# Attention over cached keys: pages transposed by VectorE in 32x32 blocks instead of by TensorE, and scores computed chunk by chunk

## The chip, the cores and the metric
The program runs on one core of a Trainium2 chip. The metric is the device time of one execution in microseconds (us); lower is better. Everything is float32.

## What is computed
One inference step of a small decoder: a pooling layer with its mixture of experts (MoE), then shared keys, values and forget gates, then one attention layer with its MoE. The prompt has 528 rows; 8 sample sequences have 4 new rows each and 2048 past rows in a paged cache of keys and values (16 pages of 128 rows, 16 heads of 64, so a page is 128 x 1024 floats, 512 KB). What the change touches is the attention of the samples over their past:

```python
s_past = jnp.einsum('nqhd,nkhd->nhqk', q, k_past).astype(jnp.float32) * ATTN_SCALE
s_past = s_past + cq - c_past.transpose(0, 2, 1)[:, :, None, :]
...
p = jax.nn.softmax(jnp.concatenate([s_past, s_new], axis=-1), axis=-1)
out = jnp.einsum('nhqk,nkhd->nqhd', p[..., :past].astype(v_past.dtype), v_past)
return out + jnp.einsum('nhqk,nkhd->nqhd', p[..., past:].astype(v_new.dtype), v_new)
```

## The kernel before, in words
The stages follow one another: pooling, MoE, projections (keys, values, queries), attention, output projection, second MoE. Each engine has its own program, and semaphores tie them together.

The attention stage is a loop `attention(i)` over the 8 samples, written out once for i = 0 and then as a hardware loop. Each round of it does three things, interleaved by hand in numbered ticks (`TICKS`, `S_TICK`, `QK_TICK`, `O_TICK` and so on say at which tick each engine writes which step):
- the front of sample i: its keys are brought into a layout in which 64 head dimensions lie on the partitions, and the scores of its 16 query rows per head group are computed and masked into `SROW`;
- the back of sample i - 1: softmax over `SROW`, transposes of the probabilities (`p_transposes`), products with the values (`values`);
- two heads of the prompt's attention (`s_step`, `t_step`, `v_step`; softmax by `pmax`, `exp`, `pnorm`; `pts` copies transposed probabilities out of PSUM).

Keys come in chunks of four pages into `KB`, which holds two chunks; values go to four slots `VSL`. SyncE (SP in the profile) issues these loads in `load_chunk`: for each page it reads the page's number from the table into a register, then issues one DMA for the 128 rows of 4 KB. `attention_loads` is a fixed order: wait until chunk ch has left `KB` (semaphore `kt_tr`), load the chunk two further on, wait for `pv_done`, load value chunk ch; the bias rows (`load_bias`) go in between. GpSimd (POOL) issues the loads of the prompt's heads (`stage`).

In `k_tick` (L1110) TensorE transposes 128x128 blocks of keys, 4 in a tick and 32 ticks a round. VectorE (`evac` on even ticks, L1933) and ScalarE (on odd ticks, L1491) copy them from PSUM to `KTR`. `qk` (L1128) multiplies them with `QBLK`, the block of queries, 256 columns at a time in four column tiles. The prompt's rows of the last tile of queries and keys go from ScalarE into `QT4` and `KT4` (parts of `KQ4`), separate from the buffer `TS` of the earlier tiles.

## Time and profile before

| | |
|---|---|
| time, median of 3 runs | 1629.07 us (1629.01 to 1629.26) |
| the profiled execution: its own time | 1625.25 us |
| its span in the profile | 1623.5 us |
| mean granted TensorE clock | 0.945 of full speed (2.4 GHz) |
| busy: PE (TensorE matmuls), DVE (VectorE), ACT (ScalarE), POOL (GpSimd) | 90%, 29%, 20%, 7% |
| DMA over the span | 424.59 MB, mean 262 GB/s |

The attention stage lies from about 662 to about 1200 us. In rows of stretches, "DMA share" is the mean busy share of the 16 DMA engines and GB/s what they moved; the rate at a full share is the one divided by the other. PEld are TensorE's weight loads, SPq and ACTq what the SyncE and ScalarE queues issue.

### The profile page before, as it was taken

The page shows a single profiled execution, that of the slowest core. Times are in us where ns is not written, and L with a number is a line of the kernel's source. Part 1 is how long each engine was busy: PE and PEld are TensorE (multiplying, and loading weights), DVE is VectorE, ACT ScalarE, POOL GpSimd, SP SyncE. Part 2 cuts the span into 40 slices and gives each one's busy share as a digit, 9 for nine tenths or more (in the row PEclk, how much of TensorE's full clock was granted, in tenths as well). Part 3 has the DMA queues.
Part 4 walks back from the last instruction along what each step waited for, and adds up shares of the span by engine and source line. Part 5 has one row for each costly group of instructions (what it writes and reads, how often), then busy time and mean ns, then how long its engine had stood idle before and what let it go on. Part 6 is the DMA issues. An engine that isn't in the chain of part 4 may idle for free.

```text
span 1623.5 us, 37862 instructions
## 1 busy us (share of the span) xinstructions
PE 1455.5 (90%) x15152; PEld 1040.5 (64%) x15152; DVE 471.8 (29%) x1112; ACT 328.7 (20%) x696; POOL 118.5 (7%) x176
## 2 busy tenths in 40 slices
PE   4988999999399999589999999999999599999991
PEld 4877988888244444356555656655545488888881
DVE  3330010000122332365545555555413301000103
ACT  2120110111111111333333434433211011110110
POOL 1012000000200000101001000000000210000002
PEclk9789999999799999799999999999998699999995
DMA  8256999999931131677988987987753069999975
GB/s 245 125 217 205 390 393 390 377 381 395 327 135 41 38 102 38 210 249 258 317 280 275 314 294 269 316 280 277 296 233 136 20 215 397 388 386 397 394 280 182
DMA packets 121996, 424.59 MB, mean 262 GB/s; under 512 B 26519, under 2 KB 40920, under 8 KB 113471
## 3 DMA queue, kind: packets, MB, share of 16 engines
q1 hardware_dynamic: 90439, 367.60, 61.8%
q0 software_dynamic: 10448, 29.73, 6.1%
q10 hardware_dynamic: 21040, 26.29, 4.7%
q8 instruction: 49, 0.80, 0.2%
q14 instruction: 20, 0.16, 0.0%
HBM read 393.70 MB, written 30.24 MB: 261 GB/s over the span
## 4 chain that ended last, share of the span: by engine, by line
PE 59%; DMA 16%; issue 14%; DVE 4%; ACT 3%; SPq 3%; POOL 1%; ACTq 1%; DVEq 0%; POOLq 0%
DMA W<-in_w_up 14%; PE PS L969 10%; PE PS L856 6%; PE PS L1110 6%; PE PS L852 6%; PE PS L887 4%; PE PS L882 4%; PE PS L1176 3%; PE PS L1128 3%; PE PS L1094 3%; PE PS L791 3%; PE PS L1055 2%; PE PS L1075 1%; DMA KB<-yd,SLi 1%; SPq L396 1%
## 5 line engine op out<-in xcount | busy, mean ns | idle before, releaser
L852 PE MATMUL PS<-W,VB 128*32 128x384 f32 x3072 | 353.2, 492 | 15.7 <-DMA W<-in_w_up 6.7
L856 PE MATMUL PS<-W,VB 128*32 128x128 f32 x3072 | 352.0, 275 | 5.5 <-issue 5.4
L856 PEld LDWEIGHTS PS<-W,VB 128*32 128x32 f32 x3072 | 335.3, 111 | 11.6 <-issue 9.6
L882 PE MATMUL PS<-W,VB 128*32 128x384 f32 x1536 | 174.7, 492 | 5.6 <-ACT VB L1326 5.6
L1110 PE MATMUL PS<-C,KB 128*128 128x128 f32 x1024 | 168.5, 296 | 9.4 <-ACT W L1491 7.7
L887 PE MATMUL PS<-W,VB 128*32 128x128 f32 (+1 forms) x1024 | 174.7, 329 | 0.0
L1110 PEld LDWEIGHTS PS<-C,KB 128*128 128x128 f32 x1024 | 118.4, 148 | 74.8 <-issue 59.8
L1755 DVE TENSOR_TENSOR VB<-VB,PS 128x384 f32<-128x384 f32 x32 | 17.7, 554 | 511.4 <-PE PS L868 470.5
L852 PEld LDWEIGHTS PS<-W,VB 128*32 128x32 f32 x3072 | 144.5, 110 | 28.8 <-DMA W<-in_w_up 12.2
L887 PEld LDWEIGHTS PS<-W,VB 128*32 128x32 f32 x1024 | 102.2, 110 | 16.0 <-issue 0.2
L1491 ACT ACTIVATE W<-PS 128x512 f32<-128x512 f32 x128 | 76.1, 595 | 169.4 <-PE PS L1110 164.2
L1933 DVE COPY W<-PS 128x512 f32<-128x512 f32 x128 | 88.1, 688 | 60.6 <-PE PS L1110 58.7
L882 PEld LDWEIGHTS PS<-W,VB 128*32 128x32 f32 x1536 | 72.4, 110 | 29.6 <-issue 20.9
L969 PE MATMUL PS<-W,VB 128*128 128x512 f32 x192 | 85.6, 603 | 1.5 <-DVE VB L1605 1.5
L1128 PE MATMUL PS<-W 128*32 128x256 f32 x1024 | 83.8, 400 | 2.2 <-DVE W L2028 1.4
L969 PE MATMUL PS<-W,KB 128*128 128x512 f32 x192 | 83.8, 593 | 0.0
L791 PE MATMUL PS<-C,VB 96*128 96x96 f32 (+2 forms) x376 | 52.7, 284 | 34.3 <-DVE VB L1586 24.0
L791 PEld LDWEIGHTS PS<-C,VB 96*128 96x128 f32 (+2 forms) x376 | 45.5, 191 | 41.9 <-DVE VB L1586 24.4
L1055 PE MATMUL PS<-W 65*128 65x128 f32 (+4 forms) x160 | 64.0, 483 | 5.4 <-DMA W<-out_v_prompt 5.4
L1094 PE MATMUL PS<-W 128*64 128x128 f32 (+2 forms) x480 | 62.6, 260 | 4.2 <-DVE W L1973 3.1
L969 PEld LDWEIGHTS PS<-W,VB 128*128 128x128 f32 x192 | 36.6, 194 | 45.5 <-issue 45.5
L1332 ACT ACTIVATE VB<-PS 128x768 f32<-128x768 f32 x32 | 26.0, 812 | 192.7 <-PE PS L887 192.7
(261 smaller groups left out, 1589.9 us busy)
## 6 DMA issues: line engine op xcount, KB each, us to landing
W<-in_w_gate SPq DMA_DIRECT2D x32, 2048.0 KB
W<-in_w_up SPq DMA_DIRECT2D x32, 2048.0 KB, 21.6
W<-in_w_down SPq DMA_DIRECT2D x32, 2048.0 KB, 11.3
KB<-in_cache_k SPq DMA_DIRECT2D x128, 512.0 KB, 5.2
W<-in_cache_v SPq DMA_DIRECT2D x64, 512.0 KB, 5.5
VB<-in_cache_v SPq DMA_DIRECT2D x64, 512.0 KB, 7.3
yd<-VB ACTq DMA_DIRECT2D x32, 288.0 KB, 7.0
W<-in_w_kvf SPq DMA_DIRECT2D x4, 2048.0 KB, 15.7
```

Source lines behind the costliest of these rows:

```text
L791: mm = pe.transpose(PS[:, bank + k // 4, (k % 4) * P:(k % 4) * P + r], s, ident[0:r, 0:r])
L852: pe.matmul(PS[32 * q:32 * q + 32, bank, 0:WIDE], x, w[:, k, 0:WIDE], start=(k == 0), stop=(k == KC - 1), tile_position=(0, 32 * q), skip_ ...
L856: mm = pe.matmul(PS[CAP:P, bank, P * q:P * q + P], x, w[:, k, WIDE:FF], start=(k == 0 and q == 0), stop=(k == KC - 1), tile_position=(0, C ...
L882: pe.matmul(PS[32 * q:32 * q + 32, 5 + n, 0:WIDE], h, w[:, f, n * WIDE:n * WIDE + WIDE], start=(f == 0), stop=(f == FC - 1), tile_position ...
L887: mm = pe.matmul(PS[CAP:P, b, at:at + n], h, w[:, f, rest + lo:rest + lo + n], start=(f == 0 and at == 0), stop=(f == FC - 1), tile_positi ...
L969: mm = pe.matmul(PS[0:r, b, :], x[:, k, 0:r], wv[s][:, k, :], start=(k == 0), stop=(k == KC - 1))
L1055: pe.matmul(PS[0:r, 6, 0:nk], QST[hh][0:DH + 1, t * P:t * P + r], KST[hh][0:DH + 1, 0:nk], start=True, stop=True)
L1094: mm = pe.matmul(out, VST[0:kr, j, vc], PTS[0:kr, j * r:(j + 1) * r], start=(j == 0), stop=(j == t), tile_position=(0, DH * hh))
L1110: mm = pe.transpose(PS[:, n % 2, (2 * x + g) * P:(2 * x + g + 1) * P], ks[:, 2 * half + g, hp * P:(hp + 1) * P], ident)
L1128: mm = pe.matmul(PS[32 * a:32 * a + 32, 2, 256 * half:256 * half + 256], QBLK[:, 2 * a + j, :], KTR[:, (2 * x + a // 2) % 4, 256 * (a % 2) ...
L1491: act.activation(KTR[:, n % 4, :], PS[:, n % 2, :], ACT.Copy).then_inc(sem("kt_odd"), 1)
L1933: dve.tensor_copy(KTR[:, n % 4, :], PS[:, n % 2, :]).then_inc(sem("kt_even"), 1)
```

## The change
- **Loads.** A key page is loaded by four DMAs instead of one. DMA a brings heads 4a to 4a + 3 (256 columns, runs of 1 KB) of all 128 rows to the 32 partitions 32a to 32a + 31; row 32c + t goes to partition t of the group, piece c. The page numbers of a chunk are read with one register load, for values too. SyncE's wait before a key load is now for the chunk's scores (`qk_done`).
- **Transposes.** `k_tick`, both `evac` and `KTR` are gone. VectorE transposes a page in place in 32x32 blocks (`keys_transposed`, 16 instructions of 128x1024 a round, on even ticks), after waiting for the whole chunk at its first page.
- **Scores.** `qk` runs once a chunk: 8 matmuls of 512 columns in four column tiles straight from `KB`, where the 128 rows of the contraction are 4 heads' 32 dimensions each, against a block-diagonal `QBLK`. The score rows of a column tile now belong to heads a, a + 4, a + 8, a + 12, and bias, values and outputs follow that order.
- **Moved.** `pts` goes from VectorE to ScalarE; `values` runs per chunk and not per page, ahead of `qk`; the output is copied twice (`OB` has 512 columns) and transposed four times instead of twice; the new rows' scores have 32 columns instead of 64.
- **Last tile.** The last tile of queries and keys uses `TS` like the others, so ScalarE waits for `ktd_out` and `qtd_out` (the stores of what `TS` held) there too. VectorE makes the samples' own `KQR` and transposes it (`K4T`, `Q4T`).

```diff
-KTICKS = 32
-QK_TICK = [2 * x + 3 for x in range(KTICKS // 2)]
+K_TICK = [2 * g for g in range(PAGES)]
+QK_TICK = (7, 15, 23, 31)
+SCORE_TICK = (8, 16, 24, 32)
-O_TICK = [g + 8 for g in range(PAGES + 1)]
+O_TICK = (7, 15, 23, 29)
...
-            def load_chunk(dst, rows, i, ch, s):
-                for g in range(CH):
-                    page = sp.value_load(pt[0:1, bass.ds(i * PAGES + ch * CH + g, 1)], min_val=0,
-                                         max_val=A["cache_k"].shape[0] - 1)
-                    sp.dma_start(dst[:, g * D:(g + 1) * D], rows[bass.ds(page * PAGE, PAGE), :]).then_inc(s, 16)
+            def load_chunk(dst, rows, i, ch, s, keys=False):
+                pages = nc.values_load_multi_w_load_instructions(
...
+                for g, page in enumerate(pages):
+                    src, to = rows[bass.ds(page * PAGE, PAGE), :], dst[:, g * D:(g + 1) * D]
+                    if keys:
+                        for a in range(4):
+                            sp.dma_start(to[32 * a:32 * a + 32, :].rearrange("p (c f) -> p c f", c=4),
+                                         src[:, 256 * a:256 * a + 256].rearrange("(c t) f -> t c f", t=32)).then_inc(s, 16)
...
-                    sp.wait_ge(sem("kt_tr"), 32 * i + 8 * (ch + 1))
+                    sp.wait_ge(sem("qk_done"), 4 * i + ch + 1)
...
-                def k_tick(n):
...
-                    for x in range(2):
-                        hp = 4 * m + 2 * x + j
-                        for g in range(2):
-                            mm = pe.transpose(PS[:, n % 2, (2 * x + g) * P:(2 * x + g + 1) * P],
-                                              ks[:, 2 * half + g, hp * P:(hp + 1) * P], ident)
-                    mm.then_inc(sem("kt_tr"), 1)
...
+                def qk(ch):
+
+                    pe.wait_ge(sem("kt_done"), 16 * i + CH * ch + CH)
...
+                    ks = KB[:, ch % 2, :].rearrange("p (x n) -> p x n", n=256)
+                    for e in range(2):
+                        for a in range(4):
+                            b = 2 * a + e
+                            mm = pe.matmul(PS[32 * a:32 * a + 32, ch % 2, :], QBLK[:, b, :], ks[:, :, 32 * b:32 * b + 32],
+                                           start=(e == 0), stop=(e == 1), tile_position=(0, 32 * a), skip_group_check=True)
...
-                dst = TS if t < 4 else QT4
-                if t < 4:
-                    act.wait_ge(sem("ktd_out"), 32 * (t + 1))
+                dst = TS
+                act.wait_ge(sem("ktd_out"), 32 * (t + 1))
...
+                def keys_transposed(g):
+
+                    ch = g // CH
+                    if g % CH == 0:
+                        dve.wait_ge(sem(f"k_in{ch % 2}"), 256 * (2 * i + ch // 2 + 1))
+                    page = KB[:, ch % 2, g % CH * D:g % CH * D + D]
+                    dve.transpose(page, page).then_inc(sem("kt_done"), 1)
```

**SyncE's queue in the hardware loop,** at the load of a key chunk. Before, each page has a register load, its checks and one DMA (two pages shown of four):

```order
L495 ISA [waits kt_tr]
L495 TENSOR_LOAD pt
L495 ISA x2
L497 ISA
L497 DMA KB<-in_cache_k 128x1024
L495 ISA
L495 TENSOR_LOAD pt
```

Now, with one register load for the chunk:

```order
L498 ISA [waits qk_done]
L498 TENSOR_LOAD pt
L505 ISA
L505 DMA KB<-in_cache_k 32x4x256
L505 ISA
L505 DMA KB<-in_cache_k 32x4x256
```

The last two rows go on until there are 16 DMAs, where there were 4; the row that waits stands in front of the value chunk and the bias rows that follow it.

**TensorE in the loop,** four ticks of it. PS is PSUM, C holds the identity, W the carved buffers (`KTR`, `QBLK`, `PR`). Before:

```order
L1110 MATMUL PS<-C,KB 128x128 [waits kt_odd]
L1110 MATMUL PS<-C,KB 128x128 x3
L1128 MATMUL PS<-W 32x256 [waits s_ready,kt_odd,kt_even]
L1128 MATMUL PS<-W 32x256 x3
L1110 MATMUL PS<-C,KB 128x128 [waits kt_even]
L1110 MATMUL PS<-C,KB 128x128 x3
L1075 MATMUL PS<-C,W 128x128 [waits pu_pts,pu_norm]
L1075 MATMUL PS<-C,W 128x128 x2
L1055 MATMUL PS<-W 128x512 [waits pu_exp]
```

Now, around the scores of a chunk:

```order
L1165 MATMUL PS<-W 32x256 x15
L1112 ISA
L176 ISA [waits qb_ready,kt_done]
L1122 MATMUL PS<-KB,W 32x512 [waits s_ready]
L1122 MATMUL PS<-KB,W 32x512 x7
L1083 REGISTER_ALU
L1087 MATMUL PS<-C,W 128x128 [waits pu_pts,pu_norm]
L1087 MATMUL PS<-C,W 128x128
L1067 MATMUL PS<-W 128x384 [waits pu_exp]
```

The L1110 rows of every tick are gone, and the score matmuls (L1128 before, L1122 now) stand in one block of 8 behind a wait for VectorE's transposes.

**VectorE in the loop,** where the last chunk of a sample begins, now:

```order
L1954 STREAM_TRANSPOSE KB<-KB 128x1024 [waits k_in1]
L1986 REGISTER_ALU
L1988 ISA [waits qk_done]
L1992 ISA [waits bias_in0]
L1994 TENSOR_TENSOR W<-PS,BIAS 128x512 [waits ptt_tr]
L1998 TENSOR_REDUCE W<-W 128x1 [waits s_ready]
L1961 REGISTER_ALU
L1964 TENSOR_REDUCE W<-PS 128x1 [waits pu_exp,pu_s]
L1954 STREAM_TRANSPOSE KB<-KB 128x1024
L1980 RECIPROCAL W<-W 128x1 [waits pu_exp]
L1982 TENSOR_SCALAR W<-W 128x512 [waits pu_rec]
```

The wait for the loaded chunk (`k_in1`) is now VectorE's, with the prompt's softmax rows (L1964 on) queued behind it; before it was TensorE's.

## Rows read from the trace of the kernel before

**Rows 1.** The page's head and its part on the 40 slices.
```profile
PE   4988999999399999589999999999999599999991
...
PEclk9789999999799999799999999999998699999995
```

**Rows 2.** Windows, one per round of the loop: busy us (count), PEclk, DMA share, GB/s.
```profile
685.90:747.80 61.90, 56.99 (x486) 38.08 (x486) 38.51 (x95) 24.75 (x63) 4.76 (x8) 0.97 0.75 257
747.80:809.60 61.80, 59.12 (x560) 35.74 (x559) 32.08 (x83) 23.21 (x58) 4.76 (x8) 0.97 0.85 281
933.40:995.30 61.90, 59.99 (x562) 36.71 (x562) 32.95 (x85) 23.19 (x58) 4.75 (x8) 0.97 0.85 294
1057.40:1119.40 62.00, 59.32 (x556) 35.31 (x554) 32.11 (x84) 23.02 (x58) 4.75 (x8) 0.97 0.85 291
```

**Rows 3.** The chain that ended last, 871 to 934 us, its first lines.
```profile
by line: PE PS L1110 21.9%; PE PS L1176 14.7%; PE PS L1128 11.8%; PE PS L1094 10.1%; PE PS L1055 9.2%; issue 7.5%; PE PS L1075 4.0%; PE PS L1158 3.5%; PE PS L1058 1.8%; DVE W L1943 1.6%; DVE W L1933 1.3%; ACT W L1501 1.3%; DVE W L1989 1.1%;
...
877.42 0.59 PE PS L1110 x4
878.01 0.57 PE PS L1128 x8
```

**Rows 4.** Groups by line and shape: out<-in, count, busy us, mean ns, idle before.
```profile
L1491 ACT ACTIVATE W<-PS 128x512 f32<-128x512 f32 x128 | 76.1, 595 | 169.4 <-PE PS L1110 164.2 <-issue 5.2
L1933 DVE COPY W<-PS 128x512 f32<-128x512 f32 x128 | 88.1, 688 | 60.6 <-PE PS L1110 58.7
```

**Rows 5.** Timeline of VectorE before the stage: start, us, what.
```profile
602.62 1.22 DVE L1877 TENSOR_TENSOR VB<-VB,kgb 128x1024 f32<-128x1024 f32 x1
```

**Rows 6.** Windows of DMA traffic; columns as in Rows 2.
```profile
604.70:606.20 1.50, 1.50 (x5) 0.64 (x4) 0.00 (x0) 0.74 (x1) 0.00 (x0) 1.00 0.86 350
606.70:609.40 2.70, 2.70 (x8) 1.24 (x7) 0.00 (x0) 0.00 (x0) 0.00 (x0) 1.00 0.82 194
646.20:647.70 1.50, 1.50 (x10) 0.57 (x8) 0.00 (x0) 1.11 (x1) 0.00 (x0) 1.00 0.65 131
665.40:666.90 1.50, 0.30 (x2) 0.30 (x3) 0.00 (x0) 0.69 (x1) 0.00 (x0) 0.50 1.00 393
350.00:400.00 50.00, 49.46 (x797) 44.33 (x796) 4.73 (x9) 5.38 (x9) 1.11 (x2) 1.00 1.00 387
10.20:13.60 3.40, 1.52 (x7) 1.55 (x8) 1.45 (x2) 0.20 (x1) 1.36 (x3) 1.00 1.09 375
```

**Rows 7.** What SyncE issues, by source line: ns min/median/max, first and last start.
```profile
L497 SPq DMA_DIRECT2D KB<-in_cache_k x128: 331/333/348, 583.6 to 1137.0; - x128
L495 SPq TENSOR_LOAD <-pt x256: 262/268/1275, 582.7 to 1166.2; - x128
L541 SPq DMA_DIRECT2D KB<-in_w_o x2: 389/396/403, 1148.4 to 1162.4; - x2
L490 SPq DMA_DIRECT2D W<-in_w_kvf x4: 540/657/4670, 395.4 to 411.4; - x4
```

**Rows 8.** Timeline of SyncE's queue in one round.
```profile
962.34 3.85 SPq L497 DMA_DIRECT2D KB<-in_cache_k  x4
967.08 3.62 SPq L497 DMA_DIRECT2D VB<-in_cache_v  x4
...
981.02 3.62 SPq L497 DMA_DIRECT2D VB<-in_cache_v  x4
985.37 3.23 SPq L506 DMA_DIRECT2D BIAS<-rpd  x4
```

**Rows 9.** The chain that ended last, where the stage begins.
```profile
665.15 0.65 ACTq L1474
665.86 0.70 ACT KQ L1413
...
667.21 8.85 DMA qtd<-KQ
```

**Rows 10.** Line L1474 (the stores of keys): from DMA to landing.
```profile
DMA to landing us min/median/max: 3.2/3.6/5.4
```

More of the change, by code:

```diff
@@ new lines, in values @@
+                    pe.wait_ge(sem("ptt_ready"), 5 * i - 5 + ch + 1)
+                    pe.wait_ge(sem(f"v_in{ch}"), 64 * i)
+                    for g in range(CH):
+                        for a in range(4):
+                            v = paged(VSL[ch])[:, g, :].rearrange("p (x a d) -> p a x d", a=4, d=DH)[:, a]
+                            mm = pe.matmul(PS[32 * a:32 * a + 32, 5, 0:256], PTT[:, CH * ch + g, 32 * a:32 * a + 32], v,
+                                           start=(ch == 0 and g == 0), stop=False, tile_position=(0, 32 * a), skip_group_check=True)
@@ new lines, in values @@
+                    mm.then_inc(sem("pv_done"), 1)
+                    if ch == NCH - 1:
+                        pe.wait_ge(sem("ptt_ready"), 5 * i)
+                        settled(pe)
+                        for a in range(4):
+                            v = V4[S0:2 * S0, :].rearrange("p (x a d) -> p a x d", a=4, d=DH)[:, a]
+                            mm = pe.matmul(PS[32 * a:32 * a + 32, 5, 0:256], PTT[S0:2 * S0, PAGES, 32 * a:32 * a + 32], v,
+                                           start=False, stop=True, tile_position=(S0, 32 * a), skip_group_check=True)
+                        mm.then_inc(sem("o_mm"), 1)
@@ L1183, in attention, with out_transposes @@
+                def out_transposes():
+                    pe.wait_ge(sem("ob_ready"), i)
+                    pe.wait_ge(sem("sn_ready"), i + 1 if front else i)
+                    settled(pe)
+                    for a in range(4):
+                        at = (P - NS) * a
+                        mm = pe.transpose(PS[:, 2 if front else 7, at:at + P], OB[:, a].rearrange("p u d -> p (u d)"), ident)
+                    mm.then_inc(sem("ob_tr"), 1)
                 for n in range(TICKS + shift):
@@ L1506, in exp, with pts @@
                             .then_inc(sem("pu_exp"), 1)
+                def pts(u):
+                    t = u % 5
+                    act.wait_ge(sem("pu_t"), 10 * i + u + 1)
+                    after(act, sem("pu_v"), 10 * i + u)
+                    if t < 4:
+                        act.activation(PTS[:, 0:P * (t + 1)], PS[:, 7, 0:P * (t + 1)], ACT.Copy).then_inc(sem("pu_pts"), 1)
+                    else:
+                        r = LASTP
+                        act.activation(PTS[:, 0:4 * r], PS[:, 7, 0:4 * r], ACT.Copy)
+                        act.activation(PTS[0:r, 4 * r:5 * r], PS[0:r, 7, 4 * r:5 * r], ACT.Copy).then_inc(sem("pu_pts"), 1)
                 def ot(u):
```

214 lines of the change are left out of this document (90 added, 124 removed).

## The prediction, on record before the changed kernel ran
> **What bounds the kernel now.** The page's forty slices show TensorE busy at nine tenths almost throughout, at a granted clock near full [rows 1]. The windows then cut the attention stage into rounds of its loop. Seven of them, from 685.9 to 1119.4 us, are 61.8 to 62.1 us long [rows 2]. In a round TensorE is busy for some 60 us, VectorE for 32.9, ScalarE for 23.2 and the DMA engines for 0.85 to 0.87 of it. So TensorE sets the pace, but DMA is only a seventh behind it. The chain of one round says the same: of it TensorE's own lines are over three quarters, the key transposes (L1110) alone 21.9%, and no transfer is named [rows 3]. Since a quicker TensorE meets the loads soon, the price of the key loads decides this change.
>
> **TensorE.** The chain gives one tick of four transposes as 0.59 us and one group of four column tiles (L1128) as 0.57 us [rows 3]. There are 32 ticks, so 18.9 us leave each round. The scores are 16 groups of 256 columns now, 9.1 us, and become 8 groups of 512 columns. As many columns pass, with half as many starts, so between 8.0 and 9.1 us; I take 8.0. TensorE's floor is 61.9 - 18.9 - 1.1 = 41.9 us a round.
>
> **VectorE and ScalarE.** The copies out of PSUM go: 16 x 0.688 = 11.0 us of VectorE and 16 x 0.595 = 9.5 us of ScalarE [rows 4]. `pts` moves, about 4.7 us. Added are 16 transposes of 128x1024. The trace has no such instruction; the nearest is the 128x1024 multiply at 1.22 us [rows 5], 19.5 us a round. Below it I see no reason; above, I allow twice it, if a 4-byte block costs two passes. VectorE comes to 32.9 - 11.0 - 4.7 + 19.5 = 36.7 us (56 at most), ScalarE to about 19. Both are covered by what follows. The position costs more than the work: VectorE waits for the whole chunk at its first page, and the prompt's softmax is queued behind that wait. A late chunk therefore stops TensorE within a tick or two.
>
> **SyncE.** A chunk's four pages take 3.6 to 3.9 us to issue, and four bias DMAs 3.2 [rows 8]. A key DMA is 0.333 us, a table load 0.268 [rows 7]. The new key DMA has 32x4x256 elements. Rows with three dimensions lie at 0.396 us (128x8x512 from w_o) and 0.54 to 0.66 us (the same shape from w_kvf) [rows 7]. I take 0.39, since w_o's steps in memory are powers of two like the cache's. With some 0.07 us of register work each, a key chunk is 16 x 0.46 + 0.6 = 8.0 us, a value chunk 4 x 0.40 + 0.6 = 2.2. The round is 4 x 10.2 + 2 x 3.2 = 47 us. At 0.66 us a DMA it is 4 x 14.5 + 6.4 = 64 us, which would be a bound of its own.
>
> **The key transfers.** A round moves 294 GB/s x 61.9 us = 18.2 MB [rows 2], of which keys are 16 x 0.524 = 8.4 MB. In a long saturated stretch 387 GB/s at a share of 1.00 pass [rows 6], so the rest, 9.8 MB, needs 25.3 us. For the keys three prices are in [rows 6], each the rate divided by the share. The best is that of the start, 10.2 to 13.6 us, where pool_w with its runs of 1 KB (256 floats) was among the traffic: 375 / 1.09 = 344 GB/s, 24.4 us. The worst is that of stores from few partitions. Storing 512 KB of keys from 128 partitions gives 350 / 0.86 = 407 GB/s; storing the same amount in two DMAs of 64 partitions each, one after the other, gives 194 / 0.82 = 237; and the 16 and 32 rows of the last tile give 131 / 0.65 = 202 GB/s, which is half. At that price keys need 41.5 us. But where such a store of 16 and 32 rows ran beside a 128-partition load, the window shows 393 GB/s at 1.00, so nothing was lost: the loss appears where all engines are in the same few partitions together. The four DMAs of a page go to four different groups, in order through one queue, and within a chunk there are sixteen. Engines that drift apart by a DMA or two are in different groups. I take the middle, 33 us. Sum 25.3 + 33.0 = 58.3 us, or 49.7 and 66.8 at the ends; with 3% of gaps, 60, 51 and 69.
>
> The trace's halved rate is what the Trainium skill, "SBUF — State Buffer", section "Door 1: The DMA port swizzle", states: 32 partitions reach 8 of 16 ports, measured there at 189 GB/s against 328, and two DMAs to the two halves don't add up. By the page alone keys would take 44 us and the round 70 us, slower than now. The 48-partition row agrees with it (202 GB/s); the mixed row is what it doesn't cover.
>
> **The ends.** In the last round the keys of a next sample aren't loaded, w_o's 4.2 MB are: 25.3 + 16.5 + 10.8 = 52.6 us, with gaps 54, so 8 us saved. At the start, ScalarE now waits for the key stores of the last tile before it scales the queries. The activation stood right behind the issue, at 665.86, and leads through an 8.85 us transfer to the first scores [rows 9]; the stores are issued until 665.80 and land in 3.2 to 5.4 us [rows 10], so between 668.4 and 670.6. Since the DMA engines were full there (share 1.00 in the fourth row of [rows 6]), I take 4 us on the chain. Everything from the output projection on is untouched.
>
> **Sum.** Six rounds (747.8 to 1119.4) x (60.1 - 61.9) = -11; first round about 0, since it waits on the same stores and loads; last round -8; start +4. That is -15 us. From the profiled execution's 1625.25 us this gives 1610; the median of the runs stands 3.8 us above that execution, so 1614 us.
>
> **Rivals.**
> - *The loads cost nothing extra.* Then keys are at 344 GB/s, DMA needs 51 us a round, SyncE 47 and TensorE 42: about 52 us. 6 x -9.9, first round -5, last -12, start +4: -72, or 1557 us. For it: the mixed row at 393 GB/s. Against it: every row in which one narrow DMA is alone.
> - *The engines stay in step and the narrow DMAs run at half rate.* The place is the key load of every chunk, 10.4 us for 2.1 MB at 202 GB/s instead of 5.2 or so. Rounds of 69 us: 6 x 7, first +7, last -4, start +4: +49, or 1678 us. It decides against the change as soon as the keys are slower than some 240 GB/s (60.0 - 25.3 = 34.7 us for 8.4 MB, the point at which a round is 61.9). For it: both narrow rows (237 and 202 GB/s) are below that. Against it: sixteen DMAs in a row, beside GpSimd's loads, give engines room to part.
> - *SyncE becomes the bound*, at 0.66 us a DMA: 64 us of issue and the waits in the same queue, 66 us a round. 7 x 4, last 0, start +4: +32, or 1661 us. For it: the w_kvf rows; against it: the w_o rows.
> - *The clock.* Where TensorE waited, between 685.9 and 809.6, the clock was still 0.97 [rows 2]. With 42 us of work in 60 it may be granted less: even at 0.75 its 42 us are 56, still covered, so this sharpens the slow cases only.
>
> **How the numbers follow.** DMA takes TensorE's place at nearly the same length: 0.34, itself 1595 to 1635. Loads cost nothing extra: 0.26. In step: 0.28. SyncE: 0.08. Others, among them VectorE's transposes at twice the price with the waits around them: 0.04. The range runs to both outer cases, 1557 to 1678; it leaves out the tips. What a measurement of this kernel can tell from no change is about 0.2%, 3 us. The middle case straddles 1629: 0.24 faster, 0.06 within, 0.04 slower. With the others: faster 0.24 + 0.26 + 0.03 = 0.53, same 0.06, slower 0.41.
>
> **What would show it.** The round's length; a DMA share near 1.0 in every round, at 300 GB/s; VectorE's waits at the first transpose of a chunk, ended by the load of the cache's keys; TensorE busy for about 42 us a round at full clock and a lower granted clock; transposes near 1.2 us; key DMAs issued at 0.39 us. If SyncE's row of sixteen is 12 us long and DMA is under 0.9, the queue was the bound. If rounds are near 52 us, narrow loads were not slow. I would be wrong in kind if a wait between VectorE, TensorE and ScalarE, and no transfer, set the round.

## The result, and the profile after

The changed kernel takes 1756.1 us (median of 4 runs, 1751.55 to 1759.8), the kernel before 1629.0 us (4 runs, 1623.0 to 1629.3). The ratio is 1.079 with a 95% interval of 1.075 to 1.083: 7.9% slower, 127 us. Forecast were 1614 us, with a range of 1560 to 1678. The profiled execution took 1751.55 us, its span is 1749.8, its mean granted clock 0.855 (before 0.945).

The page of the changed kernel, with the lines that answer to [rows 1], and the chain that ended last over the whole span:

```profile
span 1749.8 us, 34372 instructions
PE 1390.2 (79%) x13632; PEld 970.3 (55%) x13632; DVE 506.8 (29%) x1026; ACT 290.4 (17%) x672; POOL 118.8 (7%) x176
PE   4989999996799993666666767666789679999991
PEclk9789999998899996686767667776799779999996
PE 43%; DMA 19%; issue 16%; SPq 14%; DVE 4%; ACT 1%; POOL 1%; ACTq 0%; DVEq 0%; POOLq 0%
```

In the attention stage TensorE has fallen from nine tenths busy to six or seven, and its clock with it. The softmax of `SROW` by ScalarE (L1536) marks the rounds; three of them follow as windows, and below them a stretch in which little but narrow key loads (those of 32 partitions) moved, then one with value loads (all 128 partitions). Columns as in [rows 2]:

```profile
819.27:902.04 82.77, 53.70 (x371) 28.77 (x371) 36.96 (x72) 18.48 (x55) 4.75 (x8) 0.67 0.86 235
902.00:980.40 78.40, 54.20 (x371) 28.82 (x371) 36.92 (x73) 18.47 (x55) 4.65 (x9) 0.70 0.87 231
980.40:1057.80 77.40, 51.83 (x371) 27.73 (x371) 37.08 (x73) 18.47 (x55) 4.81 (x9) 0.71 0.87 226
...
921.00:926.00 5.00, 2.46 (x16) 1.76 (x14) 4.93 (x8) 1.41 (x4) 0.00 (x0) 0.91 1.07 205
935.00:939.00 4.00, 1.77 (x31) 1.40 (x31) 0.29 (x1) 1.18 (x6) 1.67 (x3) 0.97 1.03 390
```

From the second to the sixth, the rounds take 77.3 to 82.8 us where they took 61.9 to 62.9. The DMA engines are at 0.86 to 0.90, about as before, but move 226 to 235 GB/s where they moved 289 to 294: they are as busy and do less. The narrow loads pass 205 / 1.07 = 192 GB/s, the values 390 / 1.03 = 379.

The chain of one round (902 to 980.4), and SyncE's queue in it:

```profile
by line: SPq L505 32.5%; DMA KB<-in_cache_k 20.8%; issue 10.3%; PE PS L1165 8.1%; PE PS L1122 6.0%; PE PS L1106 4.8%; PE PS L1067 4.6%; PE PS L1087 2.8%; DVE W L1964 1.8%; DVE W L1994 1.7%; DVE KB L1954 1.6%; PE PS L1173 1.3%; DVE W L1982 1
...
903.51 3.92 SPq L505
...
912.08 8.08 DMA KB<-in_cache_k
920.43 0.92 issue
...
932.89 1.77 PE PS L1122 x16
935.29 0.33 SPq L505
```

```profile
899.44 12.95 SPq L505 DMA_DIRECT2D KB<-in_cache_k  x16
...
919.99 11.83 SPq L505 DMA_DIRECT2D KB<-in_cache_k  x16
932.57 1.95 SPq L508 DMA_DIRECT2D W<-in_cache_v  x4
935.29 16.69 SPq L505 DMA_DIRECT2D KB<-in_cache_k  x16
...
977.93 13.02 SPq L505 DMA_DIRECT2D KB<-in_cache_k  x16
```

In [rows 3] no transfer was on the chain. Now over half of it is the issue of key loads and their transfer, and the chain is a closed loop: a chunk is issued and lands (920.2), VectorE and TensorE work up to the end of its scores (934.7), and only then does SyncE issue the next chunk into the same half of `KB`. The issues into one half start at 899.44, 935.29 and 977.93, so two turns of 35.9 and 42.6 us make the round of 78.5.

The trace's DMA packets add one thing (a key run is a packet of 1 KB, a value row one of 4 KB). From 914 to 919 us a single DMA engine is still busy with the chunk's key packets while the others move values; exactly one key packet is under way for 26 to 29% of each of these rounds, in run 2 below for 1 to 3%. So a narrow chunk lands late also because one engine is last. Why it is last stays open.

The group of all key loads shows that an issue takes 0.317 us, but some stand for up to 5.9; and VectorE's transposes have the time forecast for them and a wait in front of them:

```profile
L505 SPq DMA_DIRECT2D KB<-in_cache_k x512: 316/317/5937, 587.4 to 1264.2; - x171
DMA to landing us min/median/max: 2.4/4.3/11.6
```

```profile
L1954 DVE STREAM_TRANSPOSE KB<-KB 128x1024 f32<-128x1024 f32 x128 | 158.2, 1236 | 101.0 <-DMA KB<-in_cache_k 100.8
```

Where the 126.3 us between the two spans lie: the first unit of the prompt starts 8.4 us later (689.43 against 680.98), the first softmax of `SROW` 17.0 us later (751.03 against 734.05), the eighth 122.8 us later (1290.45 against 1167.66), and 3.5 us come after it. Seven rounds carry 105.8 us of it.

### The profile page after: what moved, and what is told of

Read it like the earlier page. It is cut to its first block, busy times and chain, and to the rows that moved or that the text cites. A ratio compares the mean times of both kernels' runs of the same rounds, so it can differ in the third digit from the quotient of the medians.

```text
span 1749.8 us, 34372 instructions
## 1 busy us (share of the span) xinstructions
PE 1390.2 (79%) x13632; PEld 970.3 (55%) x13632; DVE 506.8 (29%) x1026; ACT 290.4 (17%) x672; POOL 118.8 (7%) x176
## 4 chain that ended last, share of the span: by engine, by line
PE 43%; DMA 19%; issue 16%; SPq 14%; DVE 4%; ACT 1%; POOL 1%; ACTq 0%; DVEq 0%; POOLq 0%
DMA W<-in_w_up 13%; SPq L505 10%; PE PS L981 10%; PE PS L868 6%; PE PS L864 5%; DMA KB<-in_cache_k 4%; PE PS L899 3%; PE PS L894 3%; PE PS L803 2%; PE PS L1122 2%; PE PS L1165 2%; PE PS L1067 1%; DVE KB L1954 1%; PE PS L1106 1%; PE PS L1087 1%
## 5 line engine op out<-in xcount | busy, mean ns | idle before, releaser
L864 PE MATMUL PS<-W,VB 128*32 128x384 f32 x3072 | 354.8, 493 | 18.4 <-DMA W<-in_w_up 8.6
L1954 DVE STREAM_TRANSPOSE KB<-KB 128x1024 f32<-128x1024 f32 x128 | 158.2, 1236 | 101.0 <-DMA KB<-in_cache_k 100.8
L1087 PE MATMUL PS<-C,W 128*128 128x128 f32 x160 | 41.6, 372 | 164.3 <-DVE W L1982 164.2
L1087 PEld LDWEIGHTS PS<-C,W 128*128 128x128 f32 x160 | 22.9, 177 | 185.2 <-DVE W L1982 173.5
L1067 PE MATMUL PS<-W 65*128 65x128 f32 (+4 forms) x160 | 87.4, 638 | 20.0 <-DMA W<-out_v_prompt 20.0
L1122 PE MATMUL PS<-KB,W 128*32 128x512 f32 x512 | 73.7, 702 | 10.6 <-DVE KB L1954 10.6
L1106 PE MATMUL PS<-W 128*64 128x128 f32 (+2 forms) x480 | 75.8, 296 | 2.9 <-ACT W L1510 2.9
L803 PEld LDWEIGHTS PS<-C,VB 96*128 96x128 f32 (+2 forms) x376 | 45.5, 191 | 41.9 <-DVE VB L1592 24.2
L1106 PEld LDWEIGHTS PS<-W 128*64 128x64 f32 (+1 forms) x480 | 54.3, 157 | 25.3 <-issue 18.5
L1964 DVE TENSOR_REDUCE W<-PS 128x1 f32<-128x128 f32 (+1 forms) x64 | 31.3, 488 | 106.4 <-PE PS L1070 106.2
```

The lines of the kernel that those rows point to most:

```text
L803: mm = pe.transpose(PS[:, bank + k // 4, (k % 4) * P:(k % 4) * P + r], s, ident[0:r, 0:r])
L864: pe.matmul(PS[32 * q:32 * q + 32, bank, 0:WIDE], x, w[:, k, 0:WIDE], start=(k == 0), stop=(k == KC - 1), tile_position=(0, 32 * q), skip_ ...
L1067: pe.matmul(PS[0:r, 6, 0:nk], QST[hh][0:DH + 1, t * P:t * P + r], KST[hh][0:DH + 1, 0:nk], start=True, stop=True)
L1087: mm = pe.transpose(PS[:, 7, j * P:(j + 1) * P], PR[:, j * P:(j + 1) * P], ident)
L1106: mm = pe.matmul(out, VST[0:kr, j, vc], PTS[0:kr, j * r:(j + 1) * r], start=(j == 0), stop=(j == t), tile_position=(0, DH * hh))
L1122: mm = pe.matmul(PS[32 * a:32 * a + 32, ch % 2, :], QBLK[:, b, :], ks[:, :, 32 * b:32 * b + 32], start=(e == 0), stop=(e == 1), tile_posit ...
```

## Experiments: what makes the key loads slow

"Wide" is a DMA that writes all 128 partitions. Ratios are against the kernel before on the same chip; the chips differ by about 1% (medians of before from 1612.6 to 1631.1 us), so ratios and rounds are compared, not times. Rounds are given from the second to the sixth.

**1. One wide DMA a page.** Keys arrive in another order, so the scores are of other values.

```diff
-                        for a in range(4):
-                            sp.dma_start(to[32 * a:32 * a + 32, :].rearrange("p (c f) -> p c f", c=4),
-                                         src[:, 256 * a:256 * a + 256].rearrange("(c t) f -> t c f", t=32)).then_inc(s, 16)
+                        sp.dma_start(to.rearrange("p (c f) -> p c f", c=4),
+                                     src.rearrange("t (x f) -> (t x) f", f=256).rearrange("(c p) f -> p c f", p=P)).then_inc(s, 16)
```

> The changed kernel with one DMA of all 128 partitions per key page, still in runs of 1 KB (the keys arrive in another order, so the scores are other numbers; the work is the same). Theory N (narrow DMAs run at half rate, and that sets the round): the key load of a chunk takes 6 us instead of 12, the round falls from 78 to about 55 us and the time to 1560 to 1590 us. Theory R (runs of 1 KB are slow in themselves): no change, 1750. Theory S (the queue's sixteen DMAs a chunk are the bound): also falls, to some 1600. Theory W (VectorE's wait in front of the prompt's softmax and the halved TensorE clock set the round, whatever the loads): stays above 1700.

Ratio 1.013 (1.007 to 1.018), rounds of 61.6 to 64.1 us. Theory N named the cause, but not the size: it had rounds of 55 us. What holds them at 62 is the subject of the second part.

**2. Four wide DMAs a page**, same count and same runs of 1 KB as the change. Keys again arrive elsewhere.

```diff
-                            sp.dma_start(to[32 * a:32 * a + 32, :].rearrange("p (c f) -> p c f", c=4),
-                                         src[:, 256 * a:256 * a + 256].rearrange("(c t) f -> t c f", t=32)).then_inc(s, 16)
+                            sp.dma_start(to[:, 256 * a:256 * a + 256], src[:, 256 * a:256 * a + 256]).then_inc(s, 16)
```

> The changed kernel with four DMAs per key page as it has, but each of all 128 partitions and 256 columns (the keys lie in another order, so the scores are other numbers). Same count of DMAs, same 1 KB runs, same bytes; only the partitions that one DMA reaches differ. Theory N: as e1, 1560 to 1590 us, with at most 10 us more. Theory S: stays at 1740 to 1760 us. Theory W: above 1700.

Ratio 1.012 (1.006 to 1.018), rounds of 61.6 to 64.1 us. Count of DMAs and length of runs are acquitted, the number of partitions is not. SyncE's stalls are gone too: the longest issue is 1.4 us.

```profile
L505 SPq DMA_DIRECT2D KB<-in_cache_k x512: 332/333/1365, 587.3 to 1165.5; - x171
```

```profile
877.74:939.61 61.87, 48.37 (x371) 26.77 (x371) 36.92 (x72) 18.47 (x56) 4.74 (x8) 0.78 0.86 284
939.61:1001.27 61.66, 48.06 (x371) 26.70 (x371) 36.94 (x72) 18.48 (x55) 4.74 (x8) 0.78 0.90 295
```

**3. Head groups in the order 0, 2, 1, 3.**

```diff
-                        for a in range(4):
+                        for a in (0, 2, 1, 3):
```

> The changed kernel with the four DMAs of a page in the order 0, 2, 1, 3, so that partitions below and above 64 alternate; the result is the reference's. Theory N with engines strictly in step: no change (each DMA is still narrow), 1745 to 1765 us. Theory N with engines that drift by a DMA: half the drift now suffices to use both halves, so 1680 to 1740 us. Theory S: no change.

Ratio 1.062 (1.057 to 1.066): 1.7 points back. Rounds of 75.1 to 78.7 us, within the band for engines that drift, though the key packets aren't much faster (213 to 242 GB/s, in the changed kernel 223 to 233).

**4. The kernel before with narrow loads:** each page in four DMAs of 32 rows of 4 KB, nothing else changed.

```diff
-                    sp.dma_start(dst[:, g * D:(g + 1) * D], rows[bass.ds(page * PAGE, PAGE), :]).then_inc(s, 16)
+                    if keys:
+                        for a in range(4):
+                            sp.dma_start(to[32 * a:32 * a + 32, :], src[32 * a:32 * a + 32, :]).then_inc(s, 16)
```

> The kernel before with each key page loaded by four DMAs of 32 partitions (rows of 4 KB, result unchanged), nothing else. Theory N: keys at about 200 GB/s need 41 us a round beside 25 us of other traffic, so rounds of 68 to 72 us and 1670 to 1710 us. Theory S: 47 us of issue a round, hidden under 62 us: 1625 to 1640 us. Theory W: 1629 us, since TensorE sets the round.

Ratio 1.057 (1.051 to 1.063), beyond the band of theory N. Its rounds (76.6 to 81.0 us) are nearly as long as the changed kernel's, with all of TensorE's old work in them and runs of 4 KB:

```profile
885.21:963.70 78.49, 66.31 (x563) 39.94 (x561) 33.27 (x85) 23.43 (x60) 4.75 (x8) 0.87 0.83 238
```

**5. 64 partitions a DMA** (0 to 63 or 64 to 127, 512 columns each; keys elsewhere).

```diff
-                            sp.dma_start(to[:, 256 * a:256 * a + 256], src[:, 256 * a:256 * a + 256]).then_inc(s, 16)
+                            h, q = 64 * (a // 2), 512 * (a % 2)
+                            sp.dma_start(to[h:h + 64, q:q + 512], src[h:h + 64, q:q + 512]).then_inc(s, 16)
```

> The kernel of four DMAs a key page, but each one 64 partitions (0 to 63 or 64 to 127) x 512 columns, in runs of 2 KB; keys arrive at other places. The order of TensorE's work is the changed kernel's. If the number of partitions sets the rate (each engine's write goes to few partitions): between the narrow kernel and the wide one, ratio 1.03 to 1.05. If 64 partitions reach the same 8 ports as 32 (the Trainium skill, "SBUF — State Buffer", section "Door 1: The DMA port swizzle"): as slow as the narrow one, ratio 1.06 to 1.08. If only the very narrow ones are slow: as the wide one, ratio 1.01 to 1.02.

Ratio 1.074 (1.072 to 1.077): as slow as 32 partitions.

**6. The middle partitions.** Again four DMAs, two of 64 partitions, but 32 to 95, and two of 32 partitions for the rest.

```diff
+                            lo, hi, q, n = ((32, 96, 0, 512), (32, 96, 512, 512), (0, 32, 0, 1024), (96, 128, 0, 1024))[a]
+                            sp.dma_start(to[lo:hi, q:q + n], src[lo:hi, q:q + n]).then_inc(s, 16)
```

> The kernel with four DMAs a key page of the same count: two of partitions 32 to 95 (64 partitions x 512 columns, runs of 2 KB) and two of partitions 0 to 31 and 96 to 127 (32 partitions x 1024 columns, 4 KB). Keys arrive at other places; TensorE's order is the changed kernel's. Partitions 0 to 63 and 64 to 127 gave a ratio of 1.074. If the number of partitions sets the rate, this is no better: 1.07 to 1.08 or more. If it is which ports they reach (the Trainium skill, "SBUF — State Buffer", section "Door 1: The DMA port swizzle", has partitions 32 to 95 reach all 16), half of the bytes go at the full rate: 1.03 to 1.055.

Ratio 1.020 (1.015 to 1.025), rounds of 61.8 to 68.5 us, below even the band of the port theory. No DMA has more partitions than in run 5, half of the bytes go in narrower ones, and 5.5 points are gone. The middle DMAs can be told by their packets of 2 KB: they go at 267 to 281 GB/s, where the narrow keys of the changed kernel go at 223 to 233 and the wide ones of run 2 at 303 to 314.

```profile
865.81:930.89 65.08, 51.30 (x371) 27.58 (x371) 36.80 (x72) 18.48 (x55) 4.74 (x8) 0.74 0.94 286
930.89:992.65 61.76, 48.26 (x371) 26.78 (x371) 37.02 (x72) 18.48 (x56) 4.74 (x8) 0.78 0.89 272
```

So which partitions a DMA covers matters, and their number alone doesn't explain it: a page in DMAs that each stay below partition 64, or above it, loads slowly (runs 4 and 5), and with half of the bytes in DMAs across that border most of the loss is gone. How fast the two outer DMAs of this run are isn't shown, since their packets have the size of value rows.

**7. Two queues.** Groups 2 and 3 from GpSimd, 0 and 1 from SyncE, so that both halves are in flight.

```diff
+                for g, page in enumerate(pages):
+                    src, to = k_rows[bass.ds(page * PAGE, PAGE), :], KB[:, slot % 2, g * D:(g + 1) * D]
+                    for a in (2, 3):
+                        pool.dma_start(to[32 * a:32 * a + 32, :].rearrange("p (c f) -> p c f", c=4),
```

> The changed kernel with its narrow key DMAs issued by two engines: head groups 0 and 1 by SyncE as before, groups 2 and 3 by GpSimd in its own queue (the first two chunks of the stage stay with SyncE). The result is the same. Theory N with halves (narrow DMAs of one queue meet in the same half of the ports, and the alternating order gave back 27 us): both halves are now in flight together, rounds fall from 78 us towards the 62 us of the wide loads, 1660 to 1700 us. Rival (each narrow DMA is slow whatever runs beside it, or GpSimd's issue takes over 1 us a DMA and 32 of them a round become the bound): 1730 us or more.

Ratio 1.076 (1.072 to 1.080): a miss for theory N with halves, in the rival's band. The DMA share went to 0.99 at 223 to 231 GB/s, so nothing idles and the transfers themselves got slower. It isn't clean evidence against the halves, since GpSimd's queue is slow by itself (run 9).

**8. Wide and in the right place, from SyncE.** DMA k carries rows 32k to 32k + 31 with all columns, spread over the four partition groups. Every word lands where the change has it. Three more kernels with the same loads were to tell apart what is left of the rounds: s_step before t_step, small transposes, and filling of TensorE (their diffs stand at runs 11 to 13, where they were made again).

```diff
-                        for a in range(4):
-                            sp.dma_start(to[32 * a:32 * a + 32, :].rearrange("p (c f) -> p c f", c=4),
-                                         src[:, 256 * a:256 * a + 256].rearrange("(c t) f -> t c f", t=32)).then_inc(s, 16)
+                        for k in range(4):
+                            sp.dma_start(to[:, 256 * k:256 * k + 256],
+                                         src[32 * k:32 * k + 32, :].rearrange("t (a f) -> a t f", a=4)).then_inc(s, 16)
```

> The changed kernel, but the four DMAs of a key page are cut by rows and not by head groups: DMA k brings rows 32k to 32k + 31, all 1024 columns, to all 128 partitions (partition 32a + t gets columns 256a to 256a + 255 of row 32k + t). Each word lands where it did; only the cut differs. Theory N (narrow DMAs halve the rate): as with the wide loads that put keys elsewhere, 1645 to 1655 us, rounds of 62 us. Rival, the scattered source (four runs of one row on different partitions) costs something: over 1670 us.

> The kernel with its key loads cut by rows, and one swap in TensorE's order: in a tick the prompt's scores of the next unit (s_step) stand ahead of the transposes of the present one (t_step), so that they and VectorE's maximum run while VectorE normalises. Theory L (what holds the rounds at 62 us is the chain s_step, maximum, exp, normalise, t_step of ten units, in series): s_step at about 0.6 us and the maximum at 0.7 leave the chain ten times a round, rounds of 50 to 56 us (the DMA engines need 55 us at 331 GB/s for 18.2 MB), 1580 to 1610 us. Theory C (TensorE's granted clock of 0.78 holds them, with 48 us of its work in 62): nothing moves, 1640 to 1655 us. Theory D (the DMA engines hold them at 0.88 of share): under 5 us of gain a round, 1615 to 1650 us.

> The kernel with its key loads cut by rows, where VectorE transposes only the first 32 columns of each page (so 31 of 32 blocks of the keys stay untransposed): 16 x 1.1 us of VectorE's work is left out of each round, the waits and signals stay. Theory L: the transposes stand between maximum and normalise or ahead of the next maximum, so a good part of the 18 us leaves the chain, rounds of 50 to 56 us, 1580 to 1610 us. Theory C or D: the rounds stay within 2 us of 62, 1635 to 1655 us.

> The kernel with its key loads cut by rows, and TensorE given four extra 128x128 transposes of a constant in each of 21 ticks of a round (84, about 12 us at full clock, into unused columns of a bank, nothing waits for them). Theory C (the low clock is what costs): TensorE waits less, its clock rises from 0.78 to over 0.9, and the rounds get no longer or even shorter, 1620 to 1655 us. Theory L: the extra work is partly in the chain, so rounds of 66 to 72 us and 1680 to 1720 us, whatever the clock does.

Ratios 1.275, 1.272, 1.272 and 1.276: all alike and far outside every theory. First the issue of key loads, then SyncE's timeline, then a window, then the DMA engines' share (tenths) and GB/s in 40 slices of 931 to 1012 us:

```profile
L505 SPq DMA_DIRECT2D KB<-in_cache_k x512: 537/1122/6685, 588.8 to 1587.8; - x171
```

```profile
931.27 24.03 SPq L505 DMA_DIRECT2D KB<-in_cache_k  x16
956.34 2.21 SPq L508 DMA_DIRECT2D W<-in_cache_v  x4
959.28 24.49 SPq L505 DMA_DIRECT2D KB<-in_cache_k  x16
```

```profile
888.98:1012.65 123.67, 52.76 (x371) 28.36 (x371) 36.96 (x72) 18.50 (x55) 4.74 (x8) 0.64 0.45 148
```

```profile
DMA  6222222226422799622222222228995222222222
GB/s 269 101 102 99 97 96 97 96 97 185 140 91 97 243 306 293 267 103 94 96 96 97 96 97 96 96 97 262 303 311 233 105 103 98 97 97 96 97 96 97
```

The rounds are 118 to 124 us long: four chunks of 24 us, values and bias. A key DMA takes 1.5 us from one to the next instead of 0.5, but SyncE's issue isn't the cause. Where keys move alone, the DMA engines stand at two tenths and 97 GB/s, a quarter of the 387 that they move when full. In the packets, exactly four are under way for 51 to 54% of a round, and almost never fewer. In the changed kernel a key DMA leaves 144 packets, 16 of them small; here it leaves 132, twelve small ones less. So each of these DMAs runs on four of the sixteen engines. Its packets are as quick as in run 2 (median 46 ns for 1 KB), and 32 of them on one engine take 1.5 us, the whole distance. The long issues (1.12 us in the median, against 0.54 to 0.65 for the first ones after a wait) are then SyncE standing behind those four. The source has four head groups as its first dimension, which fits; that this is what picks four engines wasn't tested by another cut. With four engines as the bound the three other edits had nothing to show; they say only that none of them touches it.

**9. The same DMAs from GpSimd**, with s_step first.

```diff
+                    for k in range(4):
+                        pool.dma_start(to[:, 256 * k:256 * k + 256],
+                                       src[32 * k:32 * k + 32, :].rearrange("t (a f) -> a t f", a=4))\
```

> The same result as the changed kernel. All key DMAs of the loop are issued by GpSimd, cut by rows (32 rows x 1024 columns to all 128 partitions), and s_step stands ahead of t_step in TensorE's order. On SyncE such a DMA took 1.5 us from one to the next. GpSimd took 0.55 us for a narrow one. If GpSimd is as quick for the wide ones: 64 x 0.61 = 39 us of its time a round, loads at full width, rounds of 57 to 60 us as with the wide loads and the same order, 2 to 1% faster than the kernel before. If the many-piece source costs GpSimd what it costs SyncE: 64 x 1.2 to 1.5 = 77 to 96 us a round, 15 to 28% slower.

Ratio 1.142 (1.139 to 1.144), between the two expectations and for neither reason. GpSimd issues such a DMA in 0.68 us, quickly enough, but the engines are at 0.94 to 0.97 and move only 196 to 207 GB/s:

```profile
944.22:1033.64 89.42, 51.40 (x371) 27.30 (x371) 36.91 (x72) 18.23 (x56) 47.75 (x73) 0.70 0.96 204
```

Run 11 below, with wide loads from SyncE's queue and the same order, moves 315 / 0.97 = 325 GB/s; here it is 204 / 0.96 = 212, values and all. The cut into packets differs too: 32 of 4 KB (351 ns each in this round) and 96 small ones a DMA, where run 11 has 128 of 1 KB. Whether that or the queue is the reason stays open.

## Experiments: what holds the rounds once the loads are wide

With wide loads TensorE has 48 us of work in 62, the DMA share is 0.86 to 0.92, and no wait for a key load is among the long ones. The longest waits of a round of run 2 (us in total, times, longest), apart from GpSimd's for the prompt's heads, are all links of the prompt's softmax:

```profile
ACT W L1505 <- PE PS L1086: 13.8, 6, 7.0
DVE W L1963 <- PE PS L1069: 13.1, 6, 7.0
PEld PS L1086 <- DVE W L1981: 11.8, 5, 4.7
...
ACT W L1492 <- DVE W L1963: 10.0, 8, 1.9
```

One unit in its timeline, VectorE and TensorE (start, us):

```profile
896.48 0.59 PE L1066 MATMUL PS<-W 65*128 65x512 f32 x1
...
897.70 0.68 DVE L1963 TENSOR_REDUCE W<-PS 128x1 f32<-128x512 f32 x1
898.30 1.24 DVE L1953 STREAM_TRANSPOSE KB<-KB 128x1024 f32<-128x1024 f32 x1
898.42 0.69 ACT L1492 ACTIVATE W<-PS,W 128x512 f32<-128x512 f32 x1 [1.52 <-DVE W L1963]
...
899.62 0.49 DVE L1981 TENSOR_SCALAR W<-W 128x512 f32<-128x512 f32 x1
...
900.16 0.66 PE L1086 MATMUL PS<-C,W 128*128 128x128 f32 x4 [1.48 <-DVE W L1981]
900.75 1.03 PE L1066 MATMUL PS<-W 65*16 65x512 f32 x2
```

Scores (L1066), maximum (L1963), exp (L1492), normalising (L1981), transposes (`t_step`, L1086) and only behind them the scores of the next unit: a closed chain, ten times a round, with a key transpose of 1.24 us in it.

**10. s_step first on the changed kernel, and on the kernel before** (the same swap as in run 11, with narrow loads, and with the old kernel's own).

> The changed kernel with only the order of s_step and t_step swapped on TensorE; narrow loads by SyncE. If the narrow loads alone set the rounds of 78 us: within 1% of the changed kernel, ratio 1.07 to 1.08, rounds of 76 to 78 us. If chain and loads share in it (a late chunk stops VectorE, and the time is then added to the chain): ratio 1.04 to 1.06, rounds of 71 to 75 us.

> The kernel before with only s_step and t_step swapped in TensorE's order. There TensorE is busy for 60 of 62 us of a round, and the softmax chain has room: theory L as I have it (the chain counts only where TensorE has no other work) expects 0.995 to 1.002. If the swap shortens the old kernel too, by over 0.5%, then the chain also held the kernel before, and the 62 us that both had were one cause.

Changed kernel: ratio 1.075 (1.072 to 1.079), rounds of 77.6 to 85.6 us; the loads set them. Kernel before: 1.000 (0.997 to 1.003). The order is worth nothing where TensorE is full, nor where the loads are late.

**11. s_step first, wide loads.**

```diff
+                        if m in S_TICK:
+                            s_step(S_TICK.index(m))
                         if m in T_TICK:
                             t_step(T_TICK.index(m))
-                        if m in S_TICK:
-                            s_step(S_TICK.index(m))
```

> The kernel with four wide loads a key page (all 128 partitions times 256 columns; keys reach their columns' place but not their head group's partitions, so the scores are of other keys), and one swap in TensorE's order: the prompt's scores of the next unit (s_step) ahead of the transposes of the present one (t_step). The kernel of four wide loads alone took 1648 us with rounds of 62 us. Theory L (the rounds' 62 us are the chain of ten units, s_step, maximum, exp, normalise, t_step, in series): s_step at about 0.6 us and the maximum at 0.7 leave the chain ten times a round, rounds of 54 to 57 us (DMA needs 55 us at 331 GB/s), 1590 to 1615 us. Theory C (TensorE's granted clock of 0.78 holds them): nothing moves, 1640 to 1655 us. Theory D (the DMA engines at a share of 0.88 hold them): under 3 us a round, 1625 to 1650 us.

Ratio 0.984 (0.980 to 0.988): 2.8 points off run 2, and the rounds fall to 57.2 to 58.6 us. TensorE's waits for the normalising, ahead of `t_step`, fall from 33.3 us to 1.6 in the 200 us from 850.

**12. Small key transposes, wide loads.** 31 of 32 blocks are left untransposed.

```diff
-                    dve.transpose(page, page).then_inc(sem("kt_done"), 1)
+                    dve.transpose(page[:, 0:32], page[:, 0:32]).then_inc(sem("kt_done"), 1)
```

> The kernel with four wide loads a key page, where VectorE transposes only the first 32 columns of each page (31 of 32 blocks stay untransposed): 16 x 1.1 us of VectorE's work is left out of each round, the waits and signals stay. Theory L: the key transposes stand between the maximum and the normalising of a unit, or ahead of the next maximum, so most of the 18 us leaves the chain: rounds of 54 to 57 us, 1590 to 1615 us. Theory C or D: the rounds stay within 3 us of 62, 1625 to 1655 us.

Ratio 0.986 (0.981 to 0.991), rounds of 55.0 to 58.4 us. VectorE's transposes are on the path. Like run 11 this one ends at a DMA share of 0.95 to 0.99, so neither shows all that its edit would save with quicker loads.

**13. TensorE filled, wide loads, without and with s_step first.**

```diff
+                    if front and back and 8 <= n < 29:
+                        for x in range(4):
+                            pe.transpose(PS[:, 5, 256 + P * (x % 2):384 + P * (x % 2)], ident, ident)
```

> The kernel with four wide loads a key page, and TensorE given four extra 128x128 transposes of a constant in each of 21 ticks of a round (84, about 12 us at full clock, into unused columns of a bank, nothing waits for them). Theory C (the low clock is what costs): TensorE waits less, its clock rises from 0.78 to over 0.9, and the rounds get no longer or even shorter, 1620 to 1655 us. Theory L: the extra work is partly in the chain, so rounds of 66 to 72 us, 1680 to 1720 us, whatever the clock does.

> The kernel of four wide key loads a page with s_step first (rounds of 57.6 us, ratio 0.984) and 84 extra 128x128 transposes a round on TensorE. The same filling took the wide kernel without the swap from 62.4 to 59.4 us a round. If the granted clock still costs time: the rounds stay within 57.6 us or fall to 55, ratio 0.975 to 0.985. If the chain is short enough and TensorE's own work now counts: rounds of 60 us or more, ratio 0.99 to 1.01.

Without the swap: ratio 1.001 (0.998 to 1.003), rounds of 59.2 to 60.4 us, against run 2's 61.6 to 64.1. More work made the round shorter; the chain theory alone had expected 66 to 72. With the swap: 0.991 (0.989 to 0.994), rounds of 58.0 to 58.2 us against 57.2 to 58.6, between the two cases expected. First the filled kernel, then the one with the swap, then both edits:

```profile
916.65:977.00 60.35, 52.91 (x455) 32.75 (x455) 37.09 (x72) 18.60 (x55) 4.74 (x8) 0.92 0.92 301
```

```profile
908.72:966.54 57.82, 46.41 (x371) 25.22 (x371) 36.78 (x72) 18.36 (x56) 4.74 (x8) 0.82 0.97 315
```

```profile
916.42:974.46 58.04, 51.62 (x455) 32.49 (x455) 36.85 (x72) 18.57 (x55) 4.75 (x8) 0.91 0.97 311
```

Filling raised the granted clock of a round from 0.76-0.81 to 0.89-0.92, and the steps of the chain that TensorE makes got quicker: a transpose of `t_step` has a mean of 298 ns, 333 in run 2 and 384 in the changed kernel (850 to 1050 us of each). Once the chain is short the DMA share is 0.95 to 0.99 and a higher clock gives nothing back (the filled kernel is 0.7 points the slower): the loads, wide ones, are the bound at 57 to 58 us.

## Why the prediction was wrong, step by step

- **TensorE** was to need 41.9 us a round, "at full clock and a lower granted clock". It is busy for 52 to 54 us in the changed kernel, at 0.67 to 0.72: its own work never was the bound, and what it is at full clock no run shows (44.1 us at 0.84 is the least, in run 12). The transposes of VectorE took 1.236 us (forecast 1.22), VectorE 36.9 us a round (36.7), ScalarE 18.5 (19). VectorE's and ScalarE's terms hold.
- **SyncE** was to issue a key DMA in 0.39 us with 0.07 of register work. It took 0.317 and 0.5 from one to the next: run 2 issues a chunk in 8.1 to 8.3 us, as forecast (8.0). In the changed kernel a chunk takes 11.8 to 16.8, because an issue can stand for up to 5.9 us where narrow transfers are slow. The queue isn't the cause: with as many wide DMAs it doesn't stand.
- **The key transfers are the step that failed, with the 3% of gaps.** Between 24.4 and 41.5 us I took the middle, 33, on the ground that "engines that drift apart by a DMA or two are in different groups". In the round from 902 the packets of the keys fill the DMA engines for 36.7 us (230 GB/s), all other packets for 31.8, and 10.0 are without a transfer: 78.5, where the sum had 33.0 + 25.3 + 1.8 = 60.1. Of the 18.4 us that it missed, 3.7 are the keys' own packets, 6.5 the rest of the traffic, 8.2 the gaps. The rest was priced at a full rate of 387 GB/s; with wide loads it goes at some 352 and takes 27.7 us (run 2, 1001 to 1063), beside narrow ones 31.8, because the value rows on the same engines slow down too (188 to 195 ns a row, in run 2 173 to 176). What narrow loads cost the others was no term of the sum. In the terms of the sum, with the rest at 25.3, the keys cost 43.2 us, beyond the dear end; 2.4 of that are the rate of the rest, mis-sized with wide loads too. Wide keys take 27.2 us in run 2 (309 GB/s), and the head groups in alternating order (run 3) still 35 to 39. The mixed row at 393 GB/s in [rows 6], on which the hope rested, was a small narrow store beside a wide load; sixteen narrow ones in a row are another case. Of the rows with narrow stores alone, the one at 202 GB/s is near what a stretch full of narrow loads shows (192); the one at 237, from 64 partitions and in runs of 512 B, was too high for it.
- **The gaps** come from the loop shown above: VectorE waits for the whole chunk, TensorE for it, and SyncE's next load into that half of `KB` waits for the scores. So the round isn't the sum of the transfers but two turns of that loop, and the last engine's late key packets lie in it. That a late chunk stops VectorE and TensorE was said; no time was put on it.
- **The Trainium skill**, "SBUF — State Buffer", section "Door 1: The DMA port swizzle", gave the better estimate here: 8.4 MB at its 189 GB/s are 44 us for the keys, and I went against it. The trace agrees where narrow loads fill a stretch (921 to 926 us: 192 GB/s, the key packets alone 189, for its 189); over the round the key packets go at 230. Runs 5 and 6 agree with its map, in which partitions 0 to 63 reach 8 ports and 32 to 95 all 16. What the Trainium skill says on that page under "Can I just issue two DMAs to hit both halves?", that only a transfer over all 128 partitions reaches all ports, doesn't fit run 6. The round of 70 us worked out from the page lacked the gaps too.
- **The ends.** ScalarE's wait for `ktd_out` is there (its idle time before the scaling is 5.42 us where it was 1.38, so 4.0 of the 4 forecast); as much again was already late before it, for no reason that I know. First round +8.5 (0; in the slow rival 7), last round +14 instead of -8 (74.3 us for 60.0). It doesn't get shorter by having no keys to load for a next sample: with wide loads, in run 2, the last round has 61.6 us like the others.
- **The rivals.** "In step, half rate" named the place and most of the mechanism rightly and got 0.28; its 69 us a round lacked the same gaps and the slower value rows. "Loads cost nothing extra" was priced at 52 us a round: with wide loads it was 62 (run 2, ratio 1.012), and with neither narrow loads nor the chain 57 to 58 (run 11). Its -72 us was not to be had, and half of the forecast's chance of "faster" hung on it.
- **The clock** "sharpens the slow cases only" and "still covered": the arithmetic took TensorE's work as a block. Its steps lie in a chain with VectorE's and ScalarE's, and there each is longer at 0.78 (`t_step` 333 ns for 298); run 13 gained 1.1 points by giving TensorE useless work. I had written that I would be wrong in kind if waits between the three engines set the round: in the changed kernel swapping the order gained nothing (run 10), with wide loads it did (run 11).

In points of the ratio: of 7.9, 6.7 are narrow key loads (run 2 without them is at 1.2). The remaining 1.2 aren't in the rounds: in run 2 the seven from the first softmax of `SROW` to the eighth take 434.0 us, before 433.6. There the softmax chain with the key transposes in it (at least 2.8 points by run 11 and 2.6 by run 12, which overlap; how much they share wasn't tried) happens to eat up what the loss of TensorE's own transposes, 18.9 us a round, would give. Run 10 shows that the equal 62 us have different causes. Ahead of the first softmax run 2's profile is 20.4 us longer than before's, behind the eighth 7.1; how much of that is the other chip wasn't separated.

The fastest kernel here (0.984) has its keys elsewhere; none that puts them where the layout wants them beats the kernel before. The layout that the change wants was loaded in three ways: narrow (1.079), wide from SyncE (1.275, on four DMA engines) and wide from GpSimd (1.142, slow packets). Narrow in alternating order is the best of them (1.062). Why the loads from GpSimd are slow stays open, and no cut was tried that covers all partitions, puts the keys in place and runs on all sixteen engines.

## What to carry to other kernels

Before a load is cut to suit a compute layout, look at which partitions each DMA covers and how many DMA engines its packets use, and price it by the nearest row that has the DMA alone; a mixed row is no evidence for a queue full of them. Where a buffer is loaded again only when its contents are used up, add up one turn of it: issue, landing, use. When the bound engine is relieved, write down the next two bounds and the serial chain through the small steps: what hid the chain was the work that the change removed. Here TensorE, idle for a fifth of the round, was also granted less clock (0.78 for 0.97), so part of the relief was paid back.

## What the runs showed that I had not expected

- Partitions 32 to 95 load far better than 0 to 63: ratios of 1.020 and 1.074 with four DMAs a page each, although half of the first kernel's bytes go in 32-partition DMAs.
- A load with the source in the order 4 groups x 32 rows x 256 ran on four of the sixteen DMA engines, at 97 GB/s, for the same 128 runs of 1 KB; on SyncE it looked like a slow issue (1.12 us in the median instead of 0.333).
- With narrow loads one DMA engine finished each chunk alone: for 26 to 29% of a round exactly one key packet was under way, with wide loads for 1 to 3%.
- GpSimd issues the same DMA in 0.68 us, but the transfers of a round go at 204 / 0.96 = 212 GB/s instead of 325.
- 84 useless transposes a round raised the granted clock from some 0.78 to 0.91 of 2.4 GHz and shortened the round from 62.0 us to 59.6 in the mean of seven.
